# RWKV-7 chunk core: one step of two products per inverse level instead of two dependent steps

## The reference, cut to what matters

```python
def step(state, inp):
    r_t, w_t, k_t, v_t, a_t, b_t = inp
    sa = jnp.einsum('bhvk,bhk->bhv', state, a_t)
    state = (state * w_t[:, :, None, :] + sa[..., None] * b_t[:, :, None, :]
             + v_t[..., None] * k_t[:, :, None, :])
    y_t = jnp.einsum('bhvk,bhk->bhv', state, r_t)
    return state, y_t
```

## Time and profile before

| | us |
|---|---|
| median of 3 runs | 1959.22 |
| lowest, highest | 1957.42, 1959.48 |
| profiled execution, own time | 1961.67 |
| its span, first to last instruction | 1959.6 |

### The profile page before, as it was taken

One profiled execution on the slowest core, in us unless ns is written; L12 is line 12 of the kernel. 1 busy time (PEld: TensorE's weight loads), 2 busy tenths in 40 slices (PEclk: granted clock), 3 DMA queues, 4 the chain that ended last, 5 costly groups with the idle time before them and its releaser, 6 DMA issues.

```text
span 1959.6 us, 27863 instructions
## 1 busy us (share of the span) xinstructions
PE 1920.1 (98%) x11648; PEld 1570.4 (80%) x11648; DVE 980.9 (50%) x1550; ACT 777.8 (40%) x1260; POOL 291.6 (15%) x286
## 2 busy tenths in 40 slices
PE   8999999999999999999999999999999999999997
PEld 6877777778888888887788888887888888888886
DVE  6666666556432333367645344447443432333365
ACT  6656332244443332346433333344222443232345
POOL 2001233202210010122000000014200310010124
PEclk9999999999999999999999999999999999999999
DMA  5122111135233323233322222222222242323221
GB/s 199 65 76 75 62 50 61 56 125 193 81 121 111 111 96 98 96 108 129 108 65 73 68 80 82 86 76 84 100 97 86 91 156 91 104 90 104 91 93 54
DMA packets 60080, 185.71 MB, mean 95 GB/s; under 512 B 6595, under 2 KB 11843, under 8 KB 59828
## 3 DMA queue, kind: packets, MB, share of 16 engines
q1 hardware_dynamic: 59956, 183.94, 28.2%
HBM read 173.69 MB, written 10.22 MB: 94 GB/s over the span
## 4 chain that ended last, share of the span: by engine, by line
PE 85%; DVE 6%; ACT 3%; issue 2%; POOL 2%; DMA 1%; SPq 0%; DVEq 0%; POOLq 0%; ACTq 0%
PE P L577 25%; PE P L579 25%; PE P L578 24%; DVE AREN L1766 2%; POOL AREN L2503 1%; DVE AREN L1769 1%; ACT WHI L1176 1%; DVE WLO L1773 1%; PE P L1108 1%; PE P L913 1%; PE P L766 1%; PE P L925 1%; PE P L929 1%; POOL AREN L2506 0%; PE P L1059 0%
## 5 line engine op out<-in xcount | busy, mean ns | idle before, releaser
L577 PE MATMUL P<-HH,WHI 128*128 128x512 f32 x1528 | 614.8, 402 | 5.7 <-DVE HL L1786 3.7
L579 PE MATMUL P<-HH,WLO 128*128 128x512 f32 x1528 | 597.6, 391 | 0.0
L578 PE MATMUL P<-HL,WHI 128*128 128x512 f32 x1528 | 597.0, 391 | 0.0
L1176 ACT ACTIVATE WHI<-RAW 128x1024 fp32r<-128x1024 f32 x302 | 318.0, 1054 | 421.2 <-PE P L579 420.3
L1773 DVE TENSOR_TENSOR WLO<-RAW,WHI 128x1024 fp32r<-128x1024 f32 x302 | 376.7, 1248 | 145.1 <-ACT WHI L1176 143.5
L577 PE MATMUL P<-ARR,WHI 128*128 128x512 f32 (+1 forms) x920 | 354.2, 385 | 0.0
L578 PE MATMUL P<-ARR,WHI 128*128 128x512 f32 (+1 forms) x920 | 354.1, 385 | 0.0
L579 PE MATMUL P<-ARR,WLO 128*128 128x512 f32 (+1 forms) x920 | 353.9, 385 | 0.0
L577 PEld LDWEIGHTS P<-HH,WHI 128*128 128x128 f32 x1528 | 287.7, 188 | 75.7 <-issue 6.7
L579 PEld LDWEIGHTS P<-HH,WLO 128*128 128x128 f32 x1528 | 287.4, 188 | 61.6
L578 PEld LDWEIGHTS P<-HL,WHI 128*128 128x128 f32 x1528 | 288.0, 188 | 56.3 <-issue 1.0
(11 more groups left out here) (313 smaller groups left out, 1426.4 us busy)
## 6 DMA issues: line engine op xcount, KB each, us to landing
RAW<-in_w_in_dram SPq DMA_DIRECT2D x117, 512.0 KB, 3.3
RAW<-in_w_ff_dram SPq DMA_DIRECT2D x64, 512.0 KB, 3.3
RAW<-in_w_ml_dram SPq DMA_DIRECT2D x64, 512.0 KB, 3.3
RAW<-in_w_out_dram SPq DMA_DIRECT2D x16, 512.0 KB, 3.3
RAW<-in_w_pg_dram SPq DMA_DIRECT2D x16, 512.0 KB, 3.3
AREN<-in_xT_dram SPq DMA_DIRECT2D x16, 256.0 KB, 5.8
s_gates<-AREN SPq DMA_DIRECT2D x16, 256.0 KB, 2.0
RAW<-in_w_ab_dram SPq DMA_DIRECT2D x8, 512.0 KB, 3.3
```

Of the source, the lines that this page charges most:

```text
L577: e.matmul(out, hi, H[0][:, s], start=first, stop=False)
L578: e.matmul(out, hi, H[1][:, s], start=False, stop=False)
L579: return e.matmul(out, lo, H[0][:, s], start=False, stop=last)
L1176: e.activation(WHI[n % NSPL][:, :], RAW[n % NRAW][:, :], ACT.Copy).then_inc(*D.act.sig("whi", n))
```

## The change

Each level becomes one step `V`. It keeps two matrices, `Qm` (S) and `Xm` (Y), and computes two products from them at once, each the transpose order of the other; DVE masks one into `Xm` (the mask now keeps the diagonal) and copies the other into `Qm`. POOL starts `Qm` with two adds of identity and `G` for each pair in place of four products and an add, 64x256 each. The factor 2 that the diagonal gains is taken back by ACT's scale at `W`. `V` 6 holds what `lb` 5 held. The transposed chunk products move into step `G`, in banks 6 and 7. The mean moves to `T`, the variance to `V` 2, the gate product to `V` 4, the result of the quarter before (DVE, with line 2254) to `V` 4; `front` stands at `V` 3, `V` 5, `W` and `N`. Product `N` joins step `M`, the state of chunk 2q has `N` alone, that of chunk 2q+1 joins `O`. 51 steps are spread over the same 125 rows by weights.

```diff
 def core_steps():
     out = []
     for q in range(4):
-        out += [("G", q, 0), ("T", q, 0)]
-        for lev in range(1, 6):
-            out += [("la", q, lev), ("lb", q, lev)]
-        out += [("W", q, 0), ("M", q, 0), ("N", q, 0)] + ([("S", q, 0)] if q < 3 else []) + [("O", q, 0)]
-    return out + [("E", 3, i) for i in range(3)]
+        out += [("G", q, 0, 25), ("T", q, 0, 37)]
+        out += [("V", q, lev, (22, 22, 28, 30, 24, 25)[lev - 1]) for lev in range(1, 7)]
+        out += [("W", q, 0, 25), ("M", q, 0, 25), ("N", q, 0, 22), ("O", q, 0, 25)]
+    return out + [("E", 3, i, 20) for i in range(3)]
...
+    for what, q, lev, rows in steps:
+        group = ["c", "e"] + (["f"] if q < 3 and (what in "WN" or (what, lev) in (("V", 3), ("V", 5))) else [])
+        put_steps(at, A_GA + r * 125 // n, group)
+        r += rows
...
@@ tensor_program, core
+                        o = [v3(take(6 + h)[:, 128 * jj:128 * jj + 128], 2) for h in range(2)]
+                        for j, p in jp4:
+                            for h in range(2):
+                                d = e.matmul(o[h][rws[p], j, :], AR[rws[h], j, 0, p, :], BK[rws[h], j, 3 * p, :],
+                                             start=True, stop=True)
+                        d.then_inc(*C.pe.sig("t", q))
...
+                    if what == "V" and lev < 6:
+                        marks = (C.dve.at("Y", q, 0), C.pool.at("S0", q)) if lev == 1 else (C.dve.at("S", q, lev - 1),)
+                        o = [v3(take(b, *marks)[:, 0:256], 2) for b in (b0, b1)]
+                        for i in range(2):
+                            for j, p, h in jhp:
+                                at, to = rws[p ^ (h & (lev - 1))], rws[p ^ (h & lev)]
+                                a, x = v3(Qm, 4)[at, 2 * j + h, :], v3(Xm, 4)[at, 2 * j + h, :]
+                                d = e.matmul(o[h][to, j, 64 * i:64 * i + 64], *((a, x), (x, a))[i], start=True, stop=True)
+                        d.then_inc(*C.pe.sig("v", q, lev))
+                        free[b0] = free[b1] = C.dve.at("S", q, lev)
...
-                    if what == "N":
-                        o = take(b0, C.act.at("U", q, 1))
+                        o = take(bw, C.act.at("U", q, 1))
...
-                    if what == "S":
-                        state(2 * q + 1, b0)
+                    if what == "N":
+                        state(2 * q, b1)
                     if what == "O":
+                        if q < 3:
+                            state(2 * q + 1, b0)
...
@@ scalar_program, core
+                    if what == "V" and lev == 6:
                         w.wait_ge(C.pe.at("x1", q), C.pe.at("w", q - 1))
+                        e.activation(AX[:, 0:4:2, 64:128], v3(o1[:, 0:128], 2), ACT.Copy).then_inc(*C.act.sig("x1", q, 0))
+                        w.wait_ge(C.dve.at("Q", q))
+                        e.activation(AX[:, 1:4:2, 64:128], v3(o0[:, 256:384], 2), ACT.Copy).then_inc(
+                            *C.act.sig("x1", q, 1))
...
@@ vector_program, core
                     if what == "G":
                         for h in range(2):
+                            w.wait_ge(C.pe.at("t", q), CO[1].pe.at("t", q), C.dve.at("st", 2 * q) if q else None)
+                            mul(p_.Xm_h[:, :, h, :], v3(bank(6 + h)[:, 128 * jj:128 * jj + 128], 2), lb(0, 2)).then_inc(
+                                *C.dve.sig("t", q, h))
+                        w.wait_ge(C.dve.at("t", q, 1))
+                        add(v3(Xm, 4), v3(Xm, 4), i64b).then_inc(*C.dve.sig("Y", q, 0))
+                    if what == "T":
+                        for h in range(2):
                             w.wait_ge(C.pe.at("g", q, h), C.pe.at("out", q - 1))
                             mul(v3(B_["G"], 8)[:, 4 * h:4 * h + 4, :], v3((o0, o1)[h], 4),
                                 cst("maskg").unsqueeze(1).to_broadcast([128, 4, 128])).then_inc(*C.dve.sig("gm", q, h))
...
+                    if what == "V" and lev < 6:
+                        w.wait_ge(C.pe.at("v", q, lev))
+                        mul(hj(Xm), both(b0, 128, 128)[:, :, :, 0:64], lb4(lev)).then_inc(*C.dve.sig("Y", q, lev))
+                        e.tensor_copy(hj(Qm), both(b0, 128, 64)).then_inc(*C.dve.sig("S", q, lev))
+                    if what == "V" and lev == 6:
+                        w.wait_ge(C.pe.at("x1", q))
+                        add(v3(Qm, 4), v3(o0[:, 0:256], 4), i64b).then_inc(*C.dve.sig("Q", q))
...
@@ pool_program, core
                     if what == "T":
                         for p in range(2):
-                            for h in range(2):
-                                w.wait_ge(C.dve.at("gm", q, h), ...)
-                                mul(p_.Qm_h[rws[p ^ h], :, h, :], p_.Gv[rws[p], h, :, p, 0, :],
-                                    cst("m1t")[rws[p]].unsqueeze(1).to_broadcast([64, 2, 64])).then_inc(
-                                    *C.pool.sig("q0", q, p, h))
-                        w.wait_ge(C.pool.at("q0", q, 1, 1))
-                        add(v3(p_.Qm, 4), v3(p_.Qm, 4), i64b).then_inc(*C.pool.sig("Q", q))
+                            w.wait_ge(C.dve.at("gm", q, 1), C.pe.at("w", q - 1), C.pool.at("s0", q) if p else None)
+                            add(hj(p_.Qm)[rws[p]], p_.Gv[rws[p], :, :, p, 0, :],
+                                cst("i64")[rws[p]].unsqueeze(1).unsqueeze(1).to_broadcast([64, 2, 2, 64])).then_inc(
+                                *C.pool.sig("S0" if p else "s0", q))
```

More of the change, by code:

```diff
@@ L289, in weave_order @@
         put(f"f{jj}", *rows)
[L290 to L295, removed]
+    steps, r = core_steps(), 0
+    n = sum(s[3] for s in steps)
+    for what, q, lev, rows in steps:
+        group = ["c", "e"] + (["f"] if q < 3 and (what in "WN" or (what, lev) in (("V", 3), ("V", 5))) else [])
+        put_steps(at, A_GA + r * 125 // n, group)
+        r += rows
     put("n", A_EMB2 + 8, A_HA + 2, A_HA + 7, *range(A_GL + 1, A_GL + 33, 4))
@@ L846, in second @@
                 def second(what, q, lev):
-                    if what == "la":
+                    if what == "T" and q:
+                        mean(q - 1, bw)
+                    if what == "V":
                         if lev == 1:
-                            o = take(bw, *[cc(8 + 2 * jj + j) for j in range(2)])
+                            o = take(bw, CO[0].dve.at("t", q, 1), *[cc(8 + 2 * jj + j) for j in range(2)])
                             for j in range(2):
@@ L857, in second @@
                         if lev == 2 and q:
-                            mean(q - 1, bw)
+                            variance(q - 1, bw)
                         if lev == 3:
@@ L883, in second @@
                         free[b1] = C.act.at("y", q)
-                for what, q, lev in core_steps():
+                for what, q, lev, _ in core_steps():
                     _, _, Vq, _, _, _ = p_.q(q)
@@ L901, in core @@
                             free[(b0, b1)[h]] = C.dve.at("gm", q, h)
-                    if what == "T":
-                        for h in range(2):
[L904 to L920, removed]
-                            for j in range(2):
-                                for h in range(2):
[L924 to L947, removed]
@@ new lines, in core @@
+                    if what == "V" and lev == 6:
+                        o = [take(b, C.dve.at("S", q, 5), C.act.at("vt", q, 1)) for b in (b0, b1)]
+                        xo = (o[1][:, 0:128], o[0][:, 256:384])
+                        for h in range(2):
+                            for j in range(2):
+                                for p in range(2):
+                                    e.matmul(tx(o[0][:, 0:256], j, p, h), tx(Xm, j, p, h), tx(Qm, j, p, h), start=True,
+                                             stop=True)
+                                for p in range(2):
+                                    d = e.matmul(xo[h][rws[p ^ h], 64 * j:64 * j + 64], Gu(rws[1 - p], j, p, h, 0),
+                                                 VU[rws[1 - p], j, p, 64 * h:64 * h + 64], start=True, stop=True)
+                        d.then_inc(*C.pe.sig("x1", q))
+                        free[b0], free[b1] = C.act.at("x1", q, 1), C.act.at("x1", q, 0)
@@ L948, in core @@
                     if what == "W":
-                        o = [take(b, C.dve.at("Q", q, 5), C.act.at("x1", q, 1)) for b in (b0, b1)]
+                        o = [take(b, C.dve.at("Q", q), C.act.at("x1", q, 1)) for b in (b0, b1)]
                         for j, p, h in jhp:
@@ L1552, in second @@
                 def second(what, q, lev):
-                    if what == "la" and lev == 1:
+                    if what == "V" and lev == 1:
                         w.wait_ge(C.pe.at("av", q), C.pe.at("w", q - 1))
@@ L2261, in second @@
                     Vq = p_.q(q)[2]
-                    if what == "la":
-                        if lev == 2 and q:
-                            centred(q - 1, ow)
```

(23 more changed lines are left out.)

55 lines of the change are left out of this document (17 added, 38 removed).

## The result

| | before | after | ratio, 95% interval |
|---|---|---|---|
| median, us | 1959.09 (5 runs) | 1948.81 (5 runs, 1946.84 to 1952.59) | 0.995 (0.9939 to 0.9961) |
| profiled execution, us | 1961.67 | 1952.59 | |
| its span, us | 1959.6 | 1950.8 | |

The change is worth 10.3 us, where 22 were forecast: faster, but by less than half of that, and just outside the range, whose upper end was 1948.

A forecast was written before the change was run, and what follows sets the result against it. PE was taken to bound the kernel. PE's work -20.0 us and waits of 7 against 9 (-2) gave -22 us: 1937 us for the median, 1939.7 for an execution like the profiled one; range 1930 to 1948.

The forecast's parts named there:

- What bounds the kernel, and the measure: PE, busy 98% of the span, sets the end; a step's cost is the distance between dense starts around it, less 0.47 us.
- Levels: Core levels 1 to 4: `la` and `lb` (2.55 us) become one `V` of 1.28; 16 times -1.27, -20.3 us.
- u and f: PE step prices: 16u = 0.455 us for 16 small matmuls; f = 0.365 us for leaving the dense rows and returning.
- The third rival: Row halves exclude each other in a PSUM bank: each `V` 2.19 us, 18 us more in 20 steps, 1955; chance 0.03.
- the dearer `V`: If a `V`'s quadrants overlap no better than `lb`'s, it costs 1.73 us, not 1.28: 7.2 us less gain.
- DVE's work: DVE in the core: 24 fewer operations at 0.35 us, -8 us; hidden on average, only a backlog counts.
- `G` and `M`: Moved products on PE: `T`'s add 0.455 us to each `G`; `N`'s add 1.13 to `M`, cancelled by -1.12 at `N`.
- `T`: The mean alone in quarters 1 to 3 costs 1.23 us instead of 0.86 joined: +0.37, three times +1.1.
- Waits before `V` 1: After `G`, PE waits for DVE's masks, then POOL's adds (the two stations); 4.9 us together over the quarters.
- `V` 5: Moving variance, gate product, bonus and `front`'s sum among `V` steps changes PE's work by 0.
- The 1.1 us forecast for `V` 6 in quarter 1: PE waits 1.1 us there for DVE's copy of `V` 5, late behind `front`'s part, a result and a weight split.
- The waits grow and eat half: Rival: slow POOL adds before `V` 1 (+5), `V` 5's backlog in quarters 2 and 3 (+3 to 4); 1946, chance 0.20.

## Why the prediction was wrong, and where it was right

- *What bounds the kernel, and the measure.* Right: the differences in time in these runs are those in PE's steps in the core, the clock included, and about 1 us in the merge.
- *Levels.* Right to 0.01 us, by u and f from the earlier trace rows. The third rival (row halves exclude each other in a bank) is out, the dearer `V` too. On this point the rows and the rule of the Trainium skill, "TensorEngine Tiling (Array Packing)", Gotcha 1, differ, and the measurement decides: in `V` both row halves wrote one bank at the full rate of `la`. That this rate is that of four quadrants at once is seen from the joined sum: two 128x128 matmuls of 256 columns cost 0.86 us, so 64 columns cost 0.11, and a 64x64 matmul of 64 columns in `V` costs 0.028, a quarter.
- *DVE's work.* Right: 8.5 us less. The copy out of PSUM took 0.34 us in the queue.
- *`G` and `M`.* The term was mis-sized: I added the moved products at their pure time, 16u and 1.13 us. Put behind each pair, they leave the step in four blocks with three changes of tile shape inside it, where `G`'s term had none and `M`'s one (within the 1.13). Putting like products together took away two of the three, 0.18 us each in `G` and 0.25 in `M`, 3.5 us in all. The earlier trace rows had the clue, f = 0.365 us for leaving and coming back, and I used it only at the borders of a step. For `T` the same mistake went the other way: the mean alone is of the dense shape and pays no f, 0.86 and not 1.23; the three steps `E` of before showed that.
- *Waits before `V` 1.* The mechanism was right, with its two stations, but the size was not: 4.9 us forecast, 11.2 measured, of which about 2.3 are the low clock behind quarter 0's. The waits themselves were about 3.4, 1.9, 2.1 and 1.5 us for 1.9, 1.4, 1.4 and 0.2. The adds took 0.72 us where DVE did not disturb them, as reckoned, but 1.05 and 1.59 for pair 1 of quarter 0 and 1.59 for the last one of quarter 3; I had 0.86 from the earlier trace rows for half the elements beside a busy DVE and took the faster row, though DVE is just as busy there. In quarters 1 and 2 all four adds took 0.72 to 0.74; there DVE's masks came later than reckoned: the first starts 3.2 us behind `G`'s first product and not 2.8, and pair 0's are done after 7.3 us in quarter 1 (6.2 in quarter 0), not after 5.75. And the clock was not in the sum at all, and the earlier trace rows with its 1.00 could not show it, since PE had never stood still so long there.
- *`V` 5.* The step that failed outright: "variance, gate product, bonus and `front`'s sum change places: 0". I gave them their PE time and looked for waits in the copies, not in the banks. The gate product's bank is freed by DVE's last operation of the result, 3 us later. The kernel before had the same hazard: after the gate product at `la` 5, `lb` 5 took the bank for `x1`, and the earlier trace rows show the price, 3.5 us of line 938 behind line 1766 (0.9, 0.7 and 1.3 us by the steps of quarters 1 to 3, none in quarter 0, which has no gate product). Quarter 1 of the kernel before, DVE's last operation of the result and the start of `lb` 5 right behind its end:

```profile
286.76 0.42 DVE L1766 TENSOR_TENSOR AREN<-AREN,P 128x256 f32<-128x256 f32 x1
...
287.33 0.27 PE L938 MATMUL P<-AREN 64*64 64x64 f32 x2
```

I read that row as a wait for `la`'s mask, which is of the same line, and let it vanish. The change freed `V` 6 from it and handed it to the sum at `V` 5. Cost 2.7 us in quarters 1 and 2. In quarter 0 `V` 5 waited 1.3 us for `V` 4's copy, behind `front`'s first part and a weight split, which I had worked out for quarter 1 only. The 1.1 us forecast for `V` 6 in quarter 1 did not come in either order of sum and gate product (1.74 and 1.73 us), so that term was put too high.
- *The rivals.* "The waits grow and eat half" is what happened, with its first cause right in quarters 0 and 3 (adds of 1.05 to 1.59 us beside DVE) and its second in part; its 1946 was still 3 us low, for want of the clock and the changes of shape.

## What to carry to other kernels

Where small matmuls are woven into a dense stream, a step's price is its array time plus a fixed price for every change of tile shape, within the step as well as at its ends: put products of one shape together. When a product moves to another place, look up who frees its bank and who takes the bank next, and count from the freeing instruction's end. And a wait on the engine that bounds is not only its own length: behind the some 3.4 us that PE stood still at `V` 1 of quarter 0, the half clock cost 2.3 us more.

## What the runs showed that I had not expected

- POOL's two-input add over 64 partitions and 256 elements took 0.72 us, as long as 128 partitions with the same 256 elements (0.74): halving the partitions gained nothing. It kept that 0.72 beside DVE's masks, which read PSUM, and took 1.59 beside DVE's weight split, which has two inputs from SBUF; the split grew from 1.22 to 1.74.
- The low clock after the same wait is not the same in every execution: quarter 2's `V` 1 waited 1.9 us in both profiles of the changed kernel and cost 5.36 in one and 6.82 in the other.
- A wait for POOL stands in the profile as "issue" without a releaser; only the end of POOL's block shows whose it is.
